# Some 11,800 rounded-float matmuls: each stage gives its input a distance of its own from the weight halves in SBUF

## The reference, cut to what matters

```python
def sq_relu_mlp(h, w1, w2):
    return jnp.square(jax.nn.relu(h @ w1)) @ w2
...
def swiglu(x, w_gate, w_up, w_down):
    return (jax.nn.silu(x @ w_gate) * (x @ w_up)) @ w_down
...
    for l in range(DEPTH):
        ng = norm_g[l]
        h = swiglu(rms_norm_2(x, ng[0]), ffn_w_gate[l, 0], ffn_w_up[l, 0], ffn_w_down[l, 0])
```

## Time and profile before

| | |
|---|---|
| median of 3 runs | 2286.51 us (2278.85 to 2287.15) |
| profiled execution, own time | 2287.48 us |
| its span, first to last instruction | 2285.4 us |
| mean granted TensorE clock | 0.993 of full speed |
| PE busy / weight loads busy | 2192.3 us / 1921.2 us |
| DVE busy / ACT busy | 1499.4 us / 929.3 us |

### The profile page before, as it was taken

One profiled execution on the slowest core, in us unless ns is written; L12 is line 12 of the kernel. 1 busy time (PEld: TensorE's weight loads), 2 busy tenths in 40 slices (PEclk: granted clock), 3 DMA queues, 4 the chain that ended last, 5 costly groups with the idle time before them and its releaser, 6 DMA issues.

```text
span 2285.4 us, 39544 instructions
## 1 busy us (share of the span) xinstructions
PE 2192.3 (96%) x15970; PEld 1921.2 (84%) x15970; DVE 1499.4 (66%) x2399; ACT 929.3 (41%) x1448; POOL 42.5 (2%) x37
## 2 busy tenths in 40 slices
PE   6999999999999999999999989999999999899998
PEld 3654678888778699999998988799989999688997
DVE  4789674544465766676667784576686676656666
ACT  3224532222234744454444452444454453344444
POOL 0000000000003000000002000000000000000000
PEclk9999999999999999999999998999999999999999
DMA  8768223232222055555554311355546554143553
GB/s 294 270 251 299 98 75 102 92 100 93 93 92 84 17 177 185 184 172 188 184 192 148 122 47 57 102 175 185 190 150 193 185 174 139 56 139 125 191 191 120
DMA packets 93556, 338.89 MB, mean 148 GB/s; under 512 B 10224, under 2 KB 12400, under 8 KB 93168
## 3 DMA queue, kind: packets, MB, share of 16 engines
q1 hardware_dynamic: 92096, 331.84, 43.5%
q10 hardware_dynamic: 1328, 5.21, 0.6%
HBM read 335.96 MB, written 1.05 MB: 147 GB/s over the span
## 4 chain that ended last, share of the span: by engine, by line
PE 84%; DVE 8%; ACT 4%; DMA 2%; issue 1%; SPq 0%; DVEq 0%; ACTq 0%
PE ps L556 21%; PE ps L557 21%; PE ps L558 21%; PE ps L963 2%; DMA ring<-weights 2%; PE ps L661 2%; PE ps L1234 1%; DVE WS L2058 1%; ACT HS L1827 1%; PE ps L579 1%; PE ps L1045 1%; DVE RS L2461 1%; PE ps L910 1%; PE ps L1068 1%; PE ps L920 1%
## 5 line engine op out<-in xcount | busy, mean ns | idle before, releaser
L2058 DVE TENSOR_TENSOR WS<-ring,WS 128x1024 fp32r<-128x1024 f32 x484 | 593.7, 1230 | 358.5 <-ACT WS L1514 355.1
L1514 ACT CAST WS<-ring 128x1024 fp32r<-128x1024 f32 x484 | 505.3, 1046 | 569.6 <-PE ps L558 475.3
L556 PE MATMUL ps<-HS,WS 128*128 128x256 f32 x1968 | 552.7, 281 | 3.1 <-DVE WS L2058 2.9
L558 PE MATMUL ps<-HS,WS 128*128 128x256 f32 x1968 | 548.8, 279 | 0.0
L557 PE MATMUL ps<-HS,WS 128*128 128x256 f32 x1928 | 538.1, 279 | 0.0
L556 PEld LDWEIGHTS ps<-HS,WS 128*128 128x128 f32 x1968 | 369.9, 188 | 5.5 <-DVE WS L2058 4.3
L558 PEld LDWEIGHTS ps<-HS,WS 128*128 128x128 f32 x1968 | 369.9, 188 | 0.0
L557 PEld LDWEIGHTS ps<-HS,WS 128*128 128x128 f32 x1928 | 362.4, 188 | 1.0 <-issue 1.0
L556 PE MATMUL ps<-HTS,WS 128*128 128x256 f32 x960 | 269.1, 280 | 2.9 <-DVE HTS L2138 1.6
L557 PE MATMUL ps<-HTS,WS 128*128 128x256 f32 x960 | 268.1, 279 | 0.0
L558 PE MATMUL ps<-HTS,WS 128*128 128x256 f32 x960 | 267.5, 279 | 0.0
(11 more groups left out here) (424 smaller groups left out, 3147.6 us busy)
## 6 DMA issues: line engine op xcount, KB each, us to landing
ring<-weights SPq DMA_DIRECT2D x630, 512.0 KB, 3.5
X<-xs ACTq DMA_DIRECT2D x1, 2048.0 KB, 9.0
con<-const ACTq DMA_DIRECT2D x1, 2016.0 KB, 9.5
X<-mem ACTq DMA_DIRECT2D x1, 1024.0 KB, 5.6
y<-X SPq DMA_DIRECT2D x4, 256.0 KB, 2.2
vecs<-vec SPq DMA_DIRECT2D x1, 311.5 KB, 7.7
con<-const SPq DMA_DIRECT2D x1, 130.0 KB, 8.8
```

The costliest lines, as they stand in the source:

```text
L556: pe.matmul(dst, w[0][:, cut], upper, start=first, stop=False, skip_group_check=True)
L558: return pe.matmul(dst, w[1][:, cut], upper, start=False, stop=last, skip_group_check=True)
L1514: act.copy(WS[:, split % HALVES, 0, :], ring[:, panel % RING, :]).then_inc(uppers_ready, 1)
L2058: dve.tensor_tensor(WS[:, split % HALVES, 1, :], ring[:, panel % RING, :], WS[:, split % HALVES, 0, :].bitcast(F32), ALU.subtract).then_in ...
```

## The change

No instruction, wait or shape changes: the built programs have the same instructions in the same order on every engine with the same waits, and only addresses differ. `hs_pad` goes. `HS2`, `HTS`, `CH` and `HID` become rooms that are 128 elements longer, and a stage takes its view at an offset from a table (called byte offsets, but the entries count 4-byte elements). `con_pad` keeps all that follows at a multiple of 512 bytes from where it was. Three small areas of `arena` move by 256 elements, since `HID` and `CH`, which lie under it, got longer.

```diff
-        sb("hs_pad", 8)
...
-        HS2 = sb("HS2", 2, KT, T, dt=F32R)
-        HTS = sb("HTS", 2, 2, T, dt=F32R)
+        hs_room = sb("HS2", 2 * KT * T + 128, dt=F32R)
+        hts_room = sb("HTS", 2 * 2 * T + 128, dt=F32R)
+        sb("con_pad", 8)
...
-            HID = convolution.enter_context(nc.sbuf_tensor("HID", [P, 11, 2, 2 * T], F32R))
-            CH = convolution.enter_context(nc.sbuf_tensor("CH", [P, 2, KT, 2 * T], F32R))
+            hid_room = convolution.enter_context(nc.sbuf_tensor("HID", [P, 11 * 4 * T + 128], F32R))
+            ch_room = convolution.enter_context(nc.sbuf_tensor("CH", [P, 4 * KT * T + 128], F32R))
...
+        HS_AT = {"wo": 96, "mlp1": 16, "f0": 32, "m0": 48, "f1": 28, "f2": 64, "m1": 12, "f3": 80}
+        HTS_AT = {"mlp1": 60, "f0": 12, "f1": 16, "f2": 32, "f3": 48, "m1": 0}
+        CH_AT = {"conv": 0, "pw1": 16, "pw2": 32, "mlp0": 64, "gqa": 28}
+        STAGE = {"wo": "wo", "rt": "m0", "rw": "m0", "ds": "m1", "sc": "m1"}
+
+        def hs2(tag):
+
+            return hs_room[:, HS_AT[tag]:HS_AT[tag] + 2 * KT * T].rearrange("p (a k t) -> p a k t", a=2, k=KT)
...
+        HID = hid_room[:, 80:80 + 44 * T].rearrange("p (n a t) -> p n a t", n=11, a=2)
...
-        SCP = area(19456, KT, 32)
-        chunk = CH[:, :, :, :].rearrange("p a k t -> p (a k t)")
+        SCP = area(19712, KT, 32)
+        chunk = chs("conv")[:, :, :, :].rearrange("p a k t -> p (a k t)")
...
-        YU = HS2[:, 1, :, :]
+        YU = hs2("m1")[:, 1, :, :]
...
-                                                 HS2[:, 0, k, :], HS2[:, 1, k, :], k == 0 and q == 0, k == KT - 1)
+                                                 hs2(tag)[:, 0, k, :], hs2(tag)[:, 1, k, :], k == 0 and q == 0, k == KT - 1)
```

More of the change, by code:

```diff
@@ L558, in three_products, with first_two @@
                 return pe.matmul(dst, w[1][:, cut], upper, start=False, stop=last, skip_group_check=True)
-            def first_two(dsts, starts, tag, halves=lambda half, k: HS2[:, half, k, :], sums=False):
+            def first_two(dsts, starts, tag, halves=None, sums=False):
+                halves = halves or (lambda half, k: hs2(tag)[:, half, k, :])
                 ws = split_panel(), split_panel()
@@ L587, in split_section, with split_tile @@
                 sections.append((panels[0], size))
-            def split_tile(dst, name, first=True, halves=lambda half, k: HS2[:, half, k, :]):
+            def split_tile(dst, name, first=True, halves=None):
+                halves = halves or (lambda half, k: hs2(STAGE[name[:2]])[:, half, k, :])
                 w = split_panel()
@@ L779, in _ @@
                 if kind == "up":
-                    split_tile(dst, f"mlp0_{p}", True, conv_halves)
+                    split_tile(dst, f"mlp0_{p}", True, conv_halves("mlp0"))
                     continue
@@ L818, in queries @@
                 for q in range(2):
-                    split_tile(ps[:, KQ_BANK[u], q * T:(q + 1) * T], f"kq{u}", q == 0, lambda half, k: CH[:, half, k, LAT])
+                    split_tile(ps[:, KQ_BANK[u], q * T:(q + 1) * T], f"kq{u}", q == 0, lambda half, k: chs("gqa")[:, half, k, LAT])
                     if u == KEYS and q == 0:
@@ L829, in value_rows @@
                     for t in range(4):
-                        x = [CH[:, half, k, t * P:(t + 1) * P] for half in range(2)]
+                        x = [chs("gqa")[:, half, k, t * P:(t + 1) * P] for half in range(2)]
                         dst = ps[:, 4 + t // 2, (t % 2) * T:(t % 2 + 1) * T]
@@ L1025, in split_rows @@
                     for t in range(2):
-                        x = [HS2[:, half, k, t * P:(t + 1) * P] for half in range(2)]
+                        x = [hs2("m0")[:, half, k, t * P:(t + 1) * P] for half in range(2)]
                         dst = ps[:, bank + t, :]
@@ L1531, in input_uppers @@
                     if bias:
-                        ins = act.activation(HS2[:, 0, k, :], src(k), ACT.Identity, bias=bias(k))
+                        ins = act.activation(hs2(tag)[:, 0, k, :], src(k), ACT.Identity, bias=bias(k))
                     else:
-                        ins = act.copy(HS2[:, 0, k, :], src(k))
+                        ins = act.copy(hs2(tag)[:, 0, k, :], src(k))
                     s.step(ins.then_inc(act_done, 1), f"{tag}_u{k}")
@@ L1599, in _ @@
                     part = slice(g * T, (g + 1) * T)
-                    s.step(act.activation(CH[:, 0, k, part], H[:, k, part], ACT.Identity, bias=MOD[:, k, g:g + 1],
+                    s.step(act.activation(chs("pw1")[:, 0, k, part], H[:, k, part], ACT.Identity, bias=MOD[:, k, g:g + 1],
                                           scale=GS[:, 0, k, g:g + 1]).then_inc(act_done, 1), f"pw1_u{k}")
@@ L1667, in _ @@
                     act.wait_ge(dve_done, at("dve", f"n1g{k}_{g}"))
-                    s.step(act.activation(CH[:, 0, k, part], H[:, k, part], ACT.Identity, bias=mlp_shift(0, g)(k)).then_inc(act_done, 1),
+                    s.step(act.activation(chs("mlp0")[:, 0, k, part], H[:, k, part], ACT.Identity, bias=mlp_shift(0, g)(k)).then_inc(act_done, 1),
                            f"mlp0_u{k}")
@@ L1693, in _ @@
                     act.wait_ge(dve_done, at("dve", f"n2g{k}_{g}"))
-                    s.step(act.activation(CH[:, 0, k, part], H[:, k, part], ACT.Identity, bias=MOD[:, 48 + k, g:g + 1]).then_inc(act_done, 1),
+                    s.step(act.activation(chs("gqa")[:, 0, k, part], H[:, k, part], ACT.Identity, bias=MOD[:, 48 + k, g:g + 1]).then_inc(act_done, 1),
                            f"gqa_u{k}")
@@ L1826, in pre_norm @@
                     act.wait_ge(*after(*wait(k)))
-                    s.step(act.activation(HS2[:, 0, k, :], XL(k), ACT.Identity, scale=gain(k)).then_inc(act_done, 1), f"{tag}_u{k}")
+                    s.step(act.activation(hs2(tag)[:, 0, k, :], XL(k), ACT.Identity, scale=gain(k)).then_inc(act_done, 1), f"{tag}_u{k}")
                     if k % 2:
@@ L2289, in _ @@
                     part = slice(g * T, (g + 1) * T)
-                    s.step(dve.scalar_tensor_tensor(out=CH[:, 1, k, part], in0=H[:, k, part], scalar=mod(0, 3, k, g),
-                                                    in1=CH[:, 0, k, part].bitcast(F32), op0=ALU.add,
+                    s.step(dve.scalar_tensor_tensor(out=chs("mlp0")[:, 1, k, part], in0=H[:, k, part], scalar=mod(0, 3, k, g),
+                                                    in1=chs("mlp0")[:, 0, k, part].bitcast(F32), op0=ALU.add,
                                                     op1=ALU.subtract).then_inc(dve_done, 1), f"mlp0_l{k}")
@@ L2321, in _ @@
                     part = slice(g * T, (g + 1) * T)
-                    s.step(dve.scalar_tensor_tensor(out=CH[:, 1, k, part], in0=H[:, k, part], scalar=mod(1, 0, k, g),
-                                                    in1=CH[:, 0, k, part].bitcast(F32), op0=ALU.add,
+                    s.step(dve.scalar_tensor_tensor(out=chs("gqa")[:, 1, k, part], in0=H[:, k, part], scalar=mod(1, 0, k, g),
+                                                    in1=chs("gqa")[:, 0, k, part].bitcast(F32), op0=ALU.add,
                                                     op1=ALU.subtract).then_inc(dve_done, 1), f"gqa_l{k}")
@@ L2422, in _ @@
                 two_heads = slice(2 * b, 2 * b + 2)
-                s.step(dve.tensor_tensor(HS2[:, 1, two_heads, :], GO[:, two_heads, :], HS2[:, 0, two_heads, :].bitcast(F32),
+                s.step(dve.tensor_tensor(hs2("wo")[:, 1, two_heads, :], GO[:, two_heads, :], hs2("wo")[:, 0, two_heads, :].bitcast(F32),
                                          ALU.subtract).then_inc(dve_done, 1), "go_low")
@@ L2479, in lower_inputs @@
                     dve.wait_ge(act_done, at("act", f"{tag}_u{k}"))
-                    s.step(dve.scalar_tensor_tensor(out=HS2[:, 1, k, :], in0=X[:, k, LAT], scalar=gain(k),
-                                                    in1=HS2[:, 0, k, :].bitcast(F32), op0=ALU.mult,
+                    s.step(dve.scalar_tensor_tensor(out=hs2(tag)[:, 1, k, :], in0=X[:, k, LAT], scalar=gain(k),
+                                                    in1=hs2(tag)[:, 0, k, :].bitcast(F32), op0=ALU.mult,
                                                     op1=ALU.subtract).then_inc(dve_done, 1), f"{tag}_l{k}")
```

48 lines of the change are left out of this document (26 added, 22 removed).

## The result

The changed kernel takes 2295.11 us (median of 16 runs, 2286.47 to 2297.69) against 2286.73 for the kernel before (16 runs). The ratio is 1.0033, with a 95% interval of 1.0023 to 1.0043: slower, as forecast, but by 8.4 us where I had said 17.5. That lies within the 0.5% that I had set for no change.

The account below looks back on a forecast made before the run. PE, busy 96% of the span on float32r matmuls with almost no waiting, was taken as the bound. Terms summed to +17.5 us on the profiled 2287.48, giving 2305.0, or a median of 2304.0 us; range 2249 to 2325.

Parts of the forecast that it names:

- the first rival: Distance doesn't matter off 0, or at all: 2278.4 us, or 2286.5 if gqa's 3.3 ns is the stage's; chance 0.24.
- the rule that the cost repeats with every 16 elements: Rounded-float matmuls: an input distance that is a multiple of 16 elements costs what 0 does, 120.0 ns for 256 columns.
- HS2 of wo, f0, m0, f2, f3: 3912 matmuls of 256 columns moved to multiples of 16, each from 116.7 to 120.0 ns: +12.9 us.
- HS2 of mlp1 (16): mlp1's 768 matmuls on HS2, moved to a multiple of 16, from 117.9 ns, +2.1 ns each: +1.6 us.
- HTS of f1, f2, f3: 1584 matmuls on HTS moved to multiples of 16, each +3.3 ns: +5.2 us.
- HTS of mlp1 (60): 768 matmuls on HTS in mlp1, from 117.9 to 116.7 ns at distance 60: -0.9 us.
- HTS of f0 (12), HS2 of f1 (28), m1 (12): 2048 matmuls at distances 12 past a multiple of 16, priced as 8: 0, bounds -6.8 and +6.8 us.
- CH and HID, 512 columns: 2112 matmuls moved from 0 to 16, 32, 64, 80: 0; bounds +14.6 and -7.0 us.
- gqa, 256 columns: 288 gqa matmuls moved from distance 0 to 28 and 100, off multiples of 16, -3.3 ns each: -1.0 us.
- my bounds of -3.3 and +3.3: Per 256-column matmul at 12, 28 or 60: +3.3 ns is distance 0's price, -3.3 another step from 8 downward.
- the third rival: CH and HID get slower too, 2112 matmuls at 233.8 ns: +14.6 us on top, 2318.6 us, or 2325.4; chance 0.12.
- The second rival: The tables' distances beat 8 by another 3.3 ns: 30.0 us on HS2 and HTS, -38.1 us in all, 2248.4; chance 0.25.

Follow-up runs that it names:

- the map runs: Changed kernel with other distance tables, mlp0's CH and HID at 8 and 48, then 40 and 108: 2304.85 and 2308.76 us; a third, off multiples of 4: 2322.5 us.

## Why the prediction was wrong, and where it was right

**Right.** The bound: PE is paid for each nanosecond, with no new wait (PE busy from end to end in the same windows, DVE and ACT unchanged). That the input's place against `WS` sets the pace: shown by the exchange of distances and by 28 everywhere, and, for the part of the stationary operand, by `split_rows`; the first rival falls. It isn't the only cause, as the two paces at 8 and 48 show, and mlp1's 117.9 had said so in the earlier trace rows. Costing the moved addresses of everything else at nothing: shown by the run with all distances back. One reading was too broad: in mlp0 the weight loads were busy for 207 of 250 us, not from end to end; PE was, and nothing in the sum hangs on it.

**Wrong: "I take the rule that the cost repeats with every 16 elements".** The rows that I had gave the pace at 0, 8 and, mixed, 64. 64 is indeed as slow as 0 (119.8 ns), as out_tiles had hinted, but I took one period that fits, 16, where 64 fits as well. Of the multiples of 16 only 64 was like 0 in a long stage (96 in the short `wo` was so in one execution of two); 32 was about 1 ns faster (118.6 to 118.9), 16, 48 and 80 by about 2 ns, 48 also by 6. By term, with the measured paces of both profiles:

| term | forecast, us | measured, us |
|---|---|---|
| HS2 of wo, f0, m0, f2, f3 | +12.9 | +0.4 +2.0 -0.9 +3.2 +1.2 = +5.8 |
| HS2 of mlp1 (16) | +1.6 | 0.0 |
| HTS of f1, f2, f3 | +5.2 | +0.6 +1.1 -1.6 = +0.1 |
| HTS of mlp1 (60) | -0.9 | -0.5 |
| HTS of f0 (12), HS2 of f1 (28), m1 (12) | 0 | +0.9 -3.2 +0.5 = -1.8 |
| CH and HID, 512 columns | 0 | +0.4 +0.9 +0.1 +1.7 +0.2 = +3.4 |
| gqa, 256 columns | -1.0 | -0.9 |
| split_rows | -0.3 | -0.2 |
| sum | +17.5 | +5.8 |

Each is the count times the difference of two paces, f3's HS2, for one, 1056 x (117.8 - 116.7) = +1.2; sums are of unrounded terms. The largest misses of the rule are f3, where 80 costs 117.8 and 48 113.6 instead of 120.0 for both (-0.4 us for +5.2), and m0 at 48 (-0.9 for +2.1). The distances past 12 were no class either: 12 costs 118.4, 28 113.6, 60 117.2; my bounds of -3.3 and +3.3 held for each, and I set the sum to their middle, which missed f1's HS2 by 3.2 us. f0 came out at my 118.9 to 0.5 ns only because its HS2 was faster than I said and its HTS slower. gqa's -0.9 for -1.0 is luck as well: its 192 matmuls of CH fell by 4.9 ns to 114.8, and the 96 of `value_rows`, which I had put at -3.3, didn't fall at all (119.8, 119.9). And the sign, though forecast, is what is left of terms that went both ways; more than half of it is CH and HID, which I had put at 0.

**CH and HID** took +3.4 us, between my 0 and the third rival's +14.6: that rival had the sign, and the map runs at 8, 40, 48 and 108 (233.3 to 234.3 ns) show its price of 233.8 right for other distances, but the change uses 64 and 80 in mlp0, the mildest of those measured after 0.

**The second rival**, a table better than 8, was wrong for this table and right for the kernel: 28 brings 28 us, where I had put one more step of 3.3 ns at 30.0 us. The step was a guess: no row had shown a pace below 116.6 ns.

**What the paces leave open.** 5.8 us from the paces against 8.4 between medians. The ratio's interval, 1.0023 to 1.0043, means 5.3 to 9.8 us, so the paces' sum lies inside it. What blurs it is the clock. Among the executions of one kernel the time falls as the mean granted clock rises: the changed kernel took 2297.24 us at 0.989 and 2286.47 us at 0.995. A straight line through the executions of all kernels (1.5 us for each 0.001) puts the changed kernel about 6 us above the one before at equal clock; that is an estimate, and it leaves next to nothing beside the paces. A window over m0's chain of small dependent matmuls in the changed kernel:

```profile
1370.00:1400.00 30.00, 26.11 (x695) 24.99 (x690) 17.47 (x34) 12.60 (x24) 0.00 (x0) 0.78 0.01 3
```
The same window in the run with the exchanged distances:

```profile
1370.00:1400.00 30.00, 24.71 (x642) 20.95 (x638) 17.05 (x34) 14.49 (x27) 0.00 (x0) 1.00 0.01 3
```

The granted clock (third number from the end) was 0.78 of full speed in one and 1.00 in the other, that is, part of the time at the lower of the two levels, 1.2 and 2.4 GHz. In this stretch PE does small matmuls with gaps. The stage m0 was 7.6 us shorter in the second (284.7 against 292.3 us, from its first rounded-float matmul to that of f1), of which its paces explain nothing: its distance is the same in both, and its HS2 was slower in the second (116.2 ns for 115.3). This is why single times don't rank these kernels, and why the exchanged distances gave 2286.01 us with paces that add up to +3.7 us.

## What to carry to other kernels

Where TensorE runs rounded-float products without a wait, the addresses of the stationary and the moving operand go far to set its pace: here between 113.4 and 122.2 ns for the same matmul of 256 columns. These runs show no rule to guess it by; give each stage another distance in one build, read each stage's pace from the starts, confirm by exchanging two stages and by more executions (a single stretch may show the better or the worse of two paces), and only then set the table: here the best value found, used everywhere, turned +0.3% into -1.2%. Take multiples of 16 bytes, since nothing off them came below 118.8 ns, and treat 256 and 512 columns apart, since the best distances measured differ (28 and 0).

## What the runs showed of the hardware that I had not expected

- The pace at a distance repeats with 256 bytes with few exceptions, and the best (28 elements, 112 bytes: 113.4 to 113.6 ns in all its long stages) stands beside bad ones (24: 120.0 ns, 32: 118.6 ns).
- With 512 columns in mlp0 each distance measured other than 0 and 64 costs 2 to 8 ns, though 8 is better than 0 with 256 columns.
- At distances 8 and 48 a stretch without waits keeps one of two paces (116.7 or 117.8 ns; 113.6 or 117.6 to 117.8 ns). It changed behind a wait or with the operand, and with the same kernel it came out differently in two executions (113.5 and 117.8 ns in m0).
- The Trainium skill (page "TensorE: Matmul & The Clock Gate", Part 2) has weight loads that take no read bandwidth from a running matmul, through ports of their own. By that alone one would expect one pace for all addresses. The runs disagree: 113.4 to 119.8 ns by the place of the input against `WS`, both on whole lines, and `split_rows` went from 233.3 to 228.9 ns when of its two operands only the stationary one had moved. Which part of the path clashes, if it is a clash, no run here shows.
